# Modulation weights loaded by column halves onto partition halves, their sums taken 512 columns wide

## The reference

```python
def first_block(x, c, rel_bias, ada_w, ada_b, norm_g, ...):
    c_act = jax.nn.silu(c)                                  # one row of 1024
    for i in range(DEPTH):                                  # DEPTH = 2
        mod = (c_act @ ada_w[i] + ada_b[i])[:, None, :]     # ada_w[i]: 1024 x 6144, float32
        sh_a, sc_a, g_a, sh_f, sc_f, g_f = jnp.split(mod, 6, axis=-1)
        h = rms_norm(x, norm_g[i, 0]) * (1.0 + sc_a) + sh_a
        y = moba_attention(h, ...) if i % N_MIXERS == 0 else diff_attention(h, ...)
        x = x + g_a * rms_norm(y, norm_g[i, 1])
        h = rms_norm(x, norm_g[i, 2]) * (1.0 + sc_f) + sh_f
        x = x + g_f * rms_norm(swiglu(h, ffn_w_in[i], ffn_w_out[i]), norm_g[i, 3])
    return x
```

## Time and profile before

| | us |
|---|---|
| time, median of 3 runs | 943.37 |
| lowest and highest | 942.47, 943.92 |
| profiled execution, first to last instruction (its span) | 941.5 |
| median less that span | 1.9 |
| attention 0, from its first slab's product | 39 to 119 |
| output projection 0 | 119 to 148 |
| feed-forward 0 | 150 to 345 |
| layer 1 | 345 to 650 |
| third block | 650 to 941 |

### The profile page before, as it was taken

How to read it: one execution, slowest core, us unless ns; L and a number is a source line. 1 busy time by engine, 2 the same in 40 slices (tenths; PEclk the granted TensorE clock), 3 DMA queues, 4 the chain that set the end, 5 groups by cost and what they waited for, 6 DMA issues and landing times.

```text
span 941.5 us, 14254 instructions
## 1 busy us (share of the span) xinstructions
PE 910.2 (97%) x5757; PEld 816.2 (87%) x5757; DVE 684.0 (73%) x918; ACT 512.7 (54%) x811; POOL 15.9 (2%) x63
## 2 busy tenths in 40 slices
PE   4999999999999999999999999999999999999995
PEld 2899987999999988998798888898987999999875
DVE  5889967797778777998887664566896855555556
ACT  2554547453344467878674444445893744444554
POOL 2000000000000000000010000000000000000000
PEclk9899999999999999999999999999999999999998
DMA  8999861999787845674589556663445755656511
GB/s 335 343 375 383 311 191 55 362 383 344 271 313 244 325 157 175 230 251 147 184 294 322 187 180 194 194 209 107 126 146 177 264 189 196 193 187 222 182 44 45
DMA packets 128803, 212.74 MB, mean 226 GB/s; under 512 B 7793, under 2 KB 96994, under 8 KB 128738
## 3 DMA queue, kind: packets, MB, share of 16 engines
q1 hardware_dynamic: 127234, 206.58, 64.4%
q0 software_dynamic: 1504, 5.26, 1.6%
HBM read 210.75 MB, written 1.06 MB: 225 GB/s over the span
## 4 chain that ended last, share of the span: by engine, by line
PE 84%; DVE 6%; ACT 6%; issue 1%; DMA 1%; SPq 0%; DVEq 0%; ACTq 0%
PE ps L674 24%; PE ps L675 24%; PE ps L676 24%; PE ps L725 2%; PE ps L727 2%; PE ps L733 1%; DVE w_lo L1702 1%; PE ps L951 1%; DMA ada_raw<-in_ada_w 1%; DVE w_lo L1695 1%; ACT w_hi L1221 1%; ACT w_hi L1217 1%; PE ps L812 1%; ACT yg L1268 1%; PE ps L818 0%
## 5 line engine op out<-in xcount | busy, mean ns | idle before, releaser
L1695 DVE TENSOR_TENSOR w_lo<-raw,w_hi 128x1024 fp32r<-128x1024 f32 x145 | 177.4, 1224 | 121.7 <-ACT w_hi L1217 121.5
L1217 ACT ACTIVATE w_hi<-raw 128x1024 fp32r<-128x1024 f32 x145 | 153.2, 1056 | 200.9 <-PE ps L676 174.2
L674 PE MATMUL ps<-h_hi,w_hi 128*128 128x256 f32 x912 | 259.2, 284 | 0.0
L676 PE MATMUL ps<-h_hi,w_lo 128*128 128x256 f32 x912 | 258.1, 283 | 0.0
L675 PE MATMUL ps<-h_lo,w_hi 128*128 128x256 f32 x912 | 258.0, 283 | 0.0
L1702 DVE TENSOR_TENSOR w_lo<-raw,w_hi 128x1024 fp32r<-128x1024 f32 x145 | 176.9, 1220 | 2.4 <-ACT w_hi L1221 2.1
L674 PEld LDWEIGHTS ps<-h_hi,w_hi 128*128 128x128 f32 x912 | 174.9, 192 | 1.0
L675 PEld LDWEIGHTS ps<-h_lo,w_hi 128*128 128x128 f32 x912 | 174.9, 192 | 1.0
L676 PEld LDWEIGHTS ps<-h_hi,w_lo 128*128 128x128 f32 x912 | 174.9, 192 | 0.0
L1221 ACT ACTIVATE w_hi<-raw 128x1024 fp32r<-128x1024 f32 x145 | 152.0, 1048 | 5.6 <-DMA raw<-in_ffn_w_in 1.6
L674 PE MATMUL ps<-w_hi,o_hi 128*128 128x512 f32 x264 | 104.7, 397 | 1.2 <-DVE w_lo L1702 1.1
(11 more groups left out here) (318 smaller groups left out, 1230.9 us busy)
## 6 DMA issues: line engine op xcount, KB each, us to landing
ada_raw<-in_ada_w SPq DMA_DIRECT2D x31, 1024.0 KB, 8.9
raw<-in_ffn_w_in SPq DMA_DIRECT2D x52, 512.0 KB, 6.0
raw<-in_ffn_w_out SPq DMA_DIRECT2D x44, 512.0 KB, 6.2
raw<-in_ffn_w_in SPq DMA_DIRECT2D x72, 256.0 KB, 3.9
raw<-in_w_up SPq DMA_DIRECT2D x32, 512.0 KB, 4.6
raw<-in_w_down SPq DMA_DIRECT2D x32, 512.0 KB, 4.6
raw<-in_moba_w_qkv SPq DMA_DIRECT2D x24, 512.0 KB, 9.4
raw<-in_diff_w_qkv SPq DMA_DIRECT2D x20, 512.0 KB, 5.1
```

The source lines that it names most:

```text
L674: T.matmul(out_ap, hi_s, hi_m, start=start, stop=False, skip_group_check=True)
L676: return T.matmul(out_ap, lo_s, hi_m, start=False, stop=stop, skip_group_check=True)
L1217: A.activation(w_hi[:, n.place, FRONT], raw[:, n.raw_place, FRONT], ACT.Copy).then_inc(front_hi, 1)
L1695: V.tensor_tensor(w_lo[:, n.place, FRONT], raw[:, n.raw_place, FRONT], w_hi[:, n.place, FRONT].bitcast(F32), ALU.subtract).then_inc(front_ ...
```

## The change

The first eight loads stay. Each of the 40 later loads becomes two transfers of 512 KB: one takes columns 0 to 511 of the 256 rows onto partitions 0 to 63, the other columns 512 to 1023 onto partitions 64 to 127, with four rows per partition. `ada(m)` makes four steps of 128 x 512 in place of two of 128 x 1024, with a scalar from `c_half`, in which each half of the partitions has the right values of `c_act`. A sum is then 512 wide: the lower 64 partitions hold the partial sums of the first half of the columns, the upper 64 those of the second. Slots are halves of the old ones, and layer 1's `SC_A` gets one of its own. To add up over partitions, one fp32 product of 128 columns of the sum with `half_ones` (64 columns: 32 that are one on the lower partitions, 32 on the upper) gives both halves at once, so that four products do for a vector. The three vectors of feed-forward 0 go this way too, and the splits `ada_hi` and `ada_lo` for them are gone. The gate splits take one instruction each, not two. `lam_in` shares the memory of `diag`.

```diff
@@ SP: load_ada
-                sp.dma_start(ada_place(place), rows(ada_w[l][:, ds(g * D, D)], kp)).then_inc(ada_loaded[place], 16)
+                to = ada_place(place).rearrange("p k n -> p (k n)").rearrange("p (j n) -> p j n", j=PIECES)
+                for h in range(2):
+                    src = ada_w[l][ds(kp * PIECES * HALF_P, PIECES * HALF_P), ds(g * D + h * HALF_D, HALF_D)]
+                    sp.dma_start(to[h * HALF_P:(h + 1) * HALF_P], src.rearrange("(j p) n -> p j n", p=HALF_P))\
+                        .then_inc(ada_loaded[place], 16)
@@ PE
+            def reduce_tile(bank, at, slot, t):
+
+                return T.matmul(ps[:, bank, at + 2 * WIDE * t:at + 2 * WIDE * (t + 1)], sums_of(slot)[:, t * P:(t + 1) * P],
+                                half_ones[:], start=True, stop=True, skip_group_check=True)
+
             def reduce_mods(bank, slots):
                 for s, slot in enumerate(slots):
-                    for t in range(KT):
-                        at = (s * KT + t) * WIDE
-                        last = T.matmul(ps[:, bank, at:at + WIDE], ada_sum[:, slot, t * P:(t + 1) * P], ones[:, 0:WIDE],
-                                        start=True, stop=True)
+                    for t in range(KT // 2):
+                        last = reduce_tile(bank, s * KT * WIDE, slot, t)
                 last.then_inc(ada_reduced, 1)
...
+                hi, lo = gate_split(b)
                 for c in range(2):
-                    hi, lo = gate_split(b, c)
-                    T.matmul(ps[:, banks[c]], ones_r[:], hi, start=True, stop=False, skip_group_check=True)
-                    last = T.matmul(ps[:, banks[c]], ones_r[:], lo, start=False, stop=True, skip_group_check=True)
+                    T.matmul(ps[:, banks[c]], half_ones_r[:, c], hi, start=True, stop=False, skip_group_check=True)
+                    last = T.matmul(ps[:, banks[c]], half_ones_r[:, c], lo, start=False, stop=True, skip_group_check=True)
@@ PE, feed-forward 0
                     if turns:
                         i = TURN_CHUNKS.index(chunk)
-                        pe.wait_ge(ada_lo_ready, i + 1)
+                        pe.wait_ge(ada_acc, summed(ADA_LATER + 5 * i + 4))
                         pe.wait_ge(mod_ready, i + 4)
                     def inside(quarter):
                         if turns:
-                            reduce_two(quarter)
+                            tile = reduce_tile(MISC, 0, ADA[ADA_LATER + 5 * i][4], quarter)
+                            if quarter == 3:
+                                tile.then_inc(ada_reduced, 1)
@@ ACT
             def gate_hi(b):
                 act.wait_ge(ada_acc, summed(GATE_PART[b] + 1))
-                if b == 1:
-                    act.wait_ge(ada_reduced, 7)
-                elif b == 3:
-                    act.wait_ge(slab_done, OPROJ[1] + KT // 2)
-                for c in range(2):
-                    A.activation(gate_split(b, c)[0], ada_sum[:, ADA[GATE_PART[b]][4], half(c)], ACT.Copy)\
-                        .then_inc(gate_hi_ready, 1)
+                if b % 2:
+                    act.wait_ge(slab_done, OPROJ[b // 2] + KT // 2)
+                A.activation(gate_split(b)[0], sums_of(ADA[GATE_PART[b]][4]), ACT.Copy).then_inc(gate_hi_ready, 1)
...
-            A.activation(ones_r[:], ones[:], ACT.Copy)
+            act.wait_ge(c_ready, 1)
+            for to in range(2):
+                for of in range(2):
+                    last = A.activation(c_half[to * HALF_P:(to + 1) * HALF_P, :, of],
+                                        c_act[of * HALF_P:(of + 1) * HALF_P], ACT.Copy)
+            last.then_inc(c_half_ready, 1)
...
-                        A.activation(ada_hi, ada_sum[:, SLOT_COLS], ACT.Copy).then_inc(ada_hi_ready, 1)
@@ DVE
+                if m >= FIRST_MODS:
+                    buffer = ada_place(place).rearrange("p k n -> p (k n)").rearrange("p (j n) -> p j n", j=PIECES)
+                    dve.wait_ge(ada_loaded[place], 32 * ada_turn(m))
+                    for j in range(PIECES):
+                        scalar = c_half[:, 2 * kp + j // 2, j % 2:j % 2 + 1]
+                        if kp == 0 and j == 0:
+                            V.tensor_scalar(sums_of(slot), buffer[:, j], scalar, None, ALU.mult).then_inc(ada_acc, 1)
+                        else:
+                            dve.wait_ge(ada_acc, summed(m, j))
+                            V.scalar_tensor_tensor(out=sums_of(slot), in0=buffer[:, j], scalar=scalar,
+                                                   in1=sums_of(slot), op0=ALU.mult, op1=ALU.add).then_inc(ada_acc, 1)
+                    return
...
+            for h in range(2):
+                for c in range(2):
+                    V.memset(half_ones[h * HALF_P:(h + 1) * HALF_P, c], 1.0 if h == c else 0.0)
+                    last = V.memset(half_ones_r[h * HALF_P:(h + 1) * HALF_P, c].bitcast(F32), 1.0 if h == c else 0.0)
+            last.then_inc(half_ready, 1)
...
-                        dve.wait_ge(ada_hi_ready, i + 1)
-                        V.tensor_tensor(ada_lo, ada_sum[:, SLOT_COLS], ada_hi.bitcast(F32), ALU.subtract)\
-                            .then_inc(ada_lo_ready, 1)
```

More of the change, by code:

```diff
@@ L69 @@
 FFN_MODS = (SH_A, SC_A, SH_F)
-SLOT_GF, SLOT_COLS, SLOT_GA = 0, 1, 2
+SLOT_GF, SLOT_COLS, SLOT_GA, SLOT_TURN = 0, 1, 2, 4
+HALF_P = P // 2
+PIECES = 4
 MISC = 3
@@ L110 @@
 ADA += [(0, G_A + c3, kp, c3, c3) for kp in range(4) for c3 in range(3)]
-ADA += [(l, g, kp, j % 3, SLOT_COLS if l else SLOT_GF) for j, (l, g, kp) in enumerate(
+ADA += [(l, g, kp, j % 3, (SLOT_TURN if g == SC_A else SLOT_COLS) if l else SLOT_GF) for j, (l, g, kp) in enumerate(
     [(l, g, kp) for i, later in enumerate(FFN_MODS)
@@ L309, in hidden_parts, with gate_split, sums_of, by_columns @@
             return (hid_hi[:], hid_lo[:]) if chunk == 0 else (o_hi[:, at], o_lo[:, at])
-        ada_hi, ada_lo = (o[:].rearrange("p a b -> p (a b)")[:, 0:D] for o in (o_hi, o_lo))
-        def gate_split(b, c):
+        ada_hi, ada_lo = (o[:].rearrange("p a b -> p (a b)")[:, 0:HALF_D] for o in (o_hi, o_lo))
+        def gate_split(b):
             if b % 2:
-                return ada_hi[:, c * HALF_D:(c + 1) * HALF_D], ada_lo[:, c * HALF_D:(c + 1) * HALF_D]
-            return [(small, o[:, 6:8])[c].rearrange("p a b -> p (a b)")
-                    for small, o in ((hid_hi[:], o_hi), (hid_lo[:], o_lo))]
+                return ada_hi, ada_lo
+            return [small[:].rearrange("p a b -> p (a b)") for small in (hid_hi, hid_lo)]
+        def sums_of(slot):
+            return ada_sum[:, slot % 3, half(slot // 3)]
+        def by_columns(banked):
+            return banked.rearrange("p (t h w) -> p h t w", t=KT // 2, h=2)[:, :, :, 0]
         GATE_PART = (ADA_LATER - 3, ADA_GA - 1, ADA_SCF - 1, len(ADA) - 1)
@@ L1731, in gate_lo, with mod_by_halves @@
             def gate_lo(b):
-                for c in range(2):
-                    hi, lo = gate_split(b, c)
-                    dve.wait_ge(gate_hi_ready, 2 * b + c + 1)
-                    V.tensor_tensor(lo, ada_sum[:, ADA[GATE_PART[b]][4], half(c)], hi.bitcast(F32), ALU.subtract)\
-                        .then_inc(gate_lo_ready, 1)
+                hi, lo = gate_split(b)
+                dve.wait_ge(gate_hi_ready, b + 1)
+                V.tensor_tensor(lo, sums_of(ADA[GATE_PART[b]][4]), hi.bitcast(F32), ALU.subtract)\
+                    .then_inc(gate_lo_ready, 1)
             def mod(g, sums):
                 V.tensor_tensor(mods[:, g], sums, tabA[:, g * KT:(g + 1) * KT], ALU.add).then_inc(mod_ready, 1)
+            def mod_by_halves(g, banked):
+                V.tensor_tensor(mods[:, g].rearrange("p (h t) -> p h t", h=2), by_columns(banked),
+                                tabA[:, g * KT:(g + 1) * KT].rearrange("p (h t) -> p h t", h=2), ALU.add)\
+                    .then_inc(mod_ready, 1)
             def gain_of(i, mods_done):
@@ L2143, in _ @@
                     split_lo(n + 5)
-                    if l == 0 and chunk in TURN_CHUNKS:
-                        dve.wait_ge(ada_lo_ready, i + 1)
                     if l == 0 and not last:
```

54 lines of the change are left out of this document (24 added, 30 removed).

## The result

The changed kernel takes 1026.66 us (median of 4 runs, 1017.67 to 1034.41) against 943.05 for the kernel before on the same chip (4 runs, 942.47 to 943.92): the medians lie 83.6 us apart. The ratio 1.0833, with a 95% interval of 1.0786 to 1.088, is worked out without the longest run, which fell in a slower state, and so it stands for a little less, some 79 us. The direction was forecast, 960.5 us was not, nor does the range up to 970 hold the time.

The account below looks back on a forecast made before the run. TensorE, busy 910.2 of 941.5 us, was taken as the bound, with time added only where it must wait. 943.4 less 1.8 of PE work plus 18.9 of waits for slower loads gave 960.5 us, range 937.5 to 970.

Parts of the forecast that it names:

- The direction: Whole kernel: slower than before by more than about 0.2%, chance 0.51, against 0.37 for faster and 0.12 for within it.
- 960.5 us: Whole kernel: forecast time, from 943.4 us before, less 1.8 saved on PE, plus 18.9 of waits for slower loads.
- the range up to 970: Whole kernel: range 937.5 to 970 us, its upper end taking plus 2.56 us per load.
- its price alone: Each later load, as two half transfers on 64 neighbouring partitions each: forecast plus 2.2 us, at most plus 2.56.

## What to carry to other kernels

Look where a transfer lands before its size and its runs: here 64 partitions from 0 on, or the two halves of the array in turn, loaded at 211 to 220 GB/s, every second partition or 32 to 95 at 382 and more, so choose a layout that interleaves. A slow transfer in a shared in-order queue is paid for by whatever stands behind it, and its price in the mix was nearly twice its price alone (4.2 for 2.2); let the range reach that far. Measure such a price between the same two events in both kernels, since a rate divided into the bytes of one kind leaves out what else the queue carries. Where a chain is full of transfers, read from which engine's in-order list the bound engine gets its input: the stall shows there.

## Unexpected

- Two queues used the two halves at once, 358 GB/s, where one queue that held both kinds in turn moved 220.
- The mix with half loads has two rates, 262 and then 234 to 241 GB/s, in one unchanged loop, while whole loads stay at 375 or 376 in every stretch.
- The clock at the start differs between executions. The kernels with whole loads and with every second load in the slow form issue the same work up to the first later load, but the granted clock between 30 and 40 us was 0.83 in the one and 0.50 in the other, PE busy throughout in both (and 0.90 in the changed kernel); the first slab's product came at 43.6 and 50.8 us. Whether such a delay adds to the time is not shown: in the kernel before with the new transfers that product came at 50.9 too, 7.7 us late, and its feed-forward still began at 190.29, the changed kernel's at 189.95.

```profile
30.00:40.00 10.00, 10.00 (x65) 7.74 (x63) 7.23 (x16) 7.30 (x15) 1.32 (x17) 0.83 1.01 321
...
30.00:40.00 10.00, 10.00 (x40) 7.71 (x38) 1.47 (x3) 2.11 (x2) 1.33 (x17) 0.50 0.97 303
```

- In the changed kernel the granted clock falls where PE waits (0.76 in two of the stages above, between the levels of 1.2 and 2.4 GHz), and its busy time is 23 us over that with whole loads (928.5 and 905.0). I hadn't priced this. It isn't in the sum of the loss as far as the chain shows: from 45 to 161 us and from 212 to 400 us the chain of waits holds transfers, sums and issues and no piece of PE.
